# A depthwise-convolution and attention block on Trainium2: projection, token stage and attention placed on one hand-made memory map, and the norm sums taken from rounded halves

## What is computed

```python
hx = rms_norm(x, norm_g[l]) * (1.0 + scale[:, None, :]) + shift[:, None, :]
px = split_cols(hx @ w_in[l])          # q, k, v, g_att, c_a, c_b, g_conv, f_u, g_four
q, k = rope_2d(px[0]), rope_2d(px[1]); v = px[2]
attn = windowed_attention(q, k, v, kc, vc, attn_sink[l])
u = c_a * jax.nn.sigmoid(c_b)                                  # "glu"
y = depthwise_conv(u, conv_w, 31 taps) + conv_b
y_conv = jax.nn.silu(layer_norm(y, ln_g, ln_b))                # norm over 256 channels
y = concat([attn * silu(g_att), y_conv * silu(g_conv), y_four * silu(g_four)]) @ w_out
```

## Time and profile before

| what | value |
|---|---|
| median of 3 runs | 4472.19 us (4465.35 to 4475.61) |
| the profiled execution, time | 4470.44 us |
| its span in the trace | 4468.8 us |
| TensorE busy (PE) | 3851.7 us, 86% |
| VectorE busy (DVE) | 2926.1 us, 65% |
| ScalarE busy (ACT) | 1805.5 us, 40% |
| GpSimd busy (POOL) | 1454.0 us, 33% |
| mean granted clock of TensorE | 0.931 of full speed |

### The profile page before, as it was taken

One profiled execution on the slowest core, in us unless ns is written; L12 is line 12 of the kernel. 1 busy time (PEld: TensorE's weight loads), 2 busy tenths in 40 slices (PEclk: granted clock), 3 DMA queues, 4 the chain that ended last, 5 costly groups with the idle time before them and its releaser, 6 DMA issues. The chain is left out here.

```text
span 4468.8 us, 52488 instructions
## 1 busy us (share of the span) xinstructions
PE 3851.7 (86%) x18984; PEld 3168.4 (71%) x18984; DVE 2926.1 (65%) x3915; ACT 1805.5 (40%) x3069; POOL 1454.0 (33%) x1087
## 2 busy tenths in 40 slices
PE   4669998798796999879969689998989968887998
PEld 2558886687485888678847467777777767775886
DVE  2645943687375594368835687677766669995564
ACT  3332102676221210167722236554465455554331
POOL 1421110121121111012202155554445546664554
PEclk7779999899897999989989899999999989998999
DMA  6341122422474211242146423343333356555453
GB/s 239 107 162 62 71 80 81 108 60 57 160 251 143 76 71 75 76 115 64 48 150 221 173 90 118 118 157 112 115 116 123 109 151 152 153 142 175 169 193 116
DMA packets 332386, 554.01 MB, mean 124 GB/s; under 512 B 27382, under 2 KB 212470, under 8 KB 322584
## 3 DMA queue, kind: packets, MB, share of 16 engines
q1 hardware_dynamic: 304106, 442.06, 30.9%
q0 software_dynamic: 28032, 108.72, 6.6%
HBM read 397.69 MB, written 153.00 MB: 123 GB/s over the span
## 5 line engine op out<-in xcount | busy, mean ns | idle before, releaser
L2266 PE MATMUL in_ps<-in_h,in_wp 128*128 128x512 f32 x3792 | 914.1, 402 | 98.3 <-ACT in_h L2361 36.8
L2266 PEld LDWEIGHTS in_ps<-in_h,in_wp 128*128 128x128 f32 x3792 | 731.1, 194 | 275.7 <-issue 45.7
L1832 PE MATMUL out_ps<-out_y,out_wp 128*128 128x512 f32 x2976 | 689.5, 393 | 31.0 <-ACT out_y L1682 25.2
L1832 PEld LDWEIGHTS out_ps<-out_y,out_wp 128*128 128x128 f32 x2976 | 562.3, 189 | 157.6 <-issue 29.3
L495 PE MATMUL in_ps<-h,in_wp 128*128 128x512 f32 x2880 | 653.5, 389 | 0.7 <-POOL in_wp L667 0.7
L495 PEld LDWEIGHTS in_ps<-h,in_wp 128*128 128x128 f32 x2880 | 540.4, 188 | 113.8 <-POOL in_wp L667 1.5
L2230 POOL TENSOR_TENSOR in_wp<-in_w,in_wp 128x512 fp32r<-128x512 f32 x180 | 293.4, 1630 | 280.9 <-ACT in_wp L2345 280.6
L1747 POOL TENSOR_TENSOR out_wp<-out_w,out_wp 128x2048 fp32r<-128x2048 f32 (+1 forms) x48 | 193.0, 4021 | 406.5 <-ACT out_wp L1675 406.4
L634 DVE SCALAR_TENSOR_TENSOR cy<-cu,in_cw,cy 128x2048 f32<-128x2048 f32 x120 | 314.5, 2621 | 4.3
L972 PE MATMUL att_O<-att_pT,att_vs 128*128 128x512 f32 x960 | 302.0, 423 | 0.0
L2230 POOL TENSOR_TENSOR in_wp<-in_S,in_wp 128x512 fp32r<-128x512 f32 x132 | 218.8, 1658 | 228.5 <-ACT in_wp L2345 228.5
(11 more groups left out here) (502 smaller groups left out, 6993.6 us busy)
## 6 DMA issues: line engine op xcount, KB each, us to landing
in_w<-in_w_in SPq DMA_DIRECT2D x44, 1024.0 KB, 5.4
out_w<-in_w_out SPq DMA_DIRECT2D x32, 1024.0 KB, 4.8
out_mw<-in_w_ada_rows SPq DMA_DIRECT2D x48, 512.0 KB, 3.6
gates<-in_ob SPq DMA_DIRECT2D x40, 512.0 KB, 3.0
in_w<-in_w_in SPq DMA_DIRECT2D x36, 512.0 KB, 3.5
gates<-in_ob POOLq DMA_DIRECT2D x16, 1024.0 KB, 4.2
att_qf<-q SPq DMA_DIRECT2D x64, 256.0 KB, 4.4
out_yr<-y SPq DMA_DIRECT2D x16, 1024.0 KB, 6.7
```

Source lines behind the costliest of these rows:

```text
L1832: mm = nc.tensor.matmul(ps[:, u % NB, :W], wp[:, u % NW, a, k], y[:, c % 2, b, k], start=(i + k == 0), stop=(i == 2 and k == KY - 1))
L2266: mm = nc.tensor.matmul(ps[:, i % 2, bank], wp[:, g % RING, a, k], h[:, n, b, k], start=(first and part + k == 0), stop=(part == 2 and k = ...
```

## The change

The projection, the token stage and the attention of the 2048 rows get fixed addresses from one map (`SHARED`, `PROJECT`, `TOKENS`, `ATTENTION`), so that it is known which buffer of a stage lies over which of the stage before. With a plan, an engine enters the next stage (`early`) after fewer than five others have left, and the buffers that a stage frees early are the ones that the next stage loads first.

- `project`: written out without loops. The tiles come as sigmoid, glu, sigmoid, glu, six gates, four queries, one key, two gates. The first half of the convolution starts after the first glu tile; the second glu product is taken after tap `SECOND_AT` = 16. SyncE leaves after the last rotation, VectorE when the tile before the last has been stored, TensorE when all but the last tile are emptied.
- `tokens_conformer`: VectorE makes both halves of the weights. A sum over channels is now: VectorE adds the two halves of channels, rounds the sum (`totA`), subtracts (`totB`), and TensorE takes two matmuls of rounded operands. Sums, squares and Silu stand behind the tokens that four written-out lists name.
- `attention`: POOL issues the first keys, queries, mask and sink, VectorE makes both halves of the first ones; values and the rest are loaded by SyncE after it has left the token stage.
- Code of `project` for kinds of tiles that no call uses is removed. The columns of `w_in` are reordered on the host to fit.
- The context's stages get no plan, but run the same functions: unrolled, in the new order, with the new sums.

The core of the diff:

```diff
+HALF = 32768
+SHARED = placed((0, ("h", 4 * HALF), ("cy", 16384), ("cu", 16640)))
+PROJECT = placed((SHARED["cu"] + 16640, ("rot", 4096), ("w1", 4096), ("wp1", 8192), ("ob1", 8192), ("w0", 4096), ("wp0", 8192), ("ob0", 8192),
+                  ("cw31", 256), ("cb31", 32)))
+TOKENS = placed((SHARED["cu"], ("wA", 12288), ("w", 6144)), (SHARED["cu"] + 12288, ("tot", 2048), ("totA", 2048), ("totB", 2048)),
+                (PROJECT["w1"], ("wB", 12288), ("ob", 6144), ("root", 2048)),
+                (PROJECT["w0"], ("rstd", 4096), ("xh", 8192), ("sg", 8192)),
+                (PROJECT["cw31"] + 288, ("ones", 512), ("eps", 32), ("par", 32)))
+ATTENTION = placed((0, ("qf", 8192), ("qs", 8192), ("kf", 20480), ("kA", 20480), ("kB", 20480), ("mk", 7680), ("vf", 10240),
+                    ("ident", 512), ("nsink", 64), ("nm", 64), ("den", 64), ("sx", 64), ("rden", 64)),
+                   (3 * HALF, ("vs", 30720)),
+                   (4 * HALF, ("prob", 40960), ("pT", 16384), ("g", 4096), ("o", 4096), ("gR", 4096), ("wide", 4096)))
...
-                        with eng.Fori(start, end, 1) as i:
-                            for q in range(2):
-                                tile(i + at, q, kind, i * 2 + q, out, i * 2 + (n0 + q), scale)
...
+            def weights(t):
+                wait(sp, parted, t - 1)
+                sp.dma_start(wt[t % 2][:], w[t]).then_inc(w_in[t % 2], 16)
...
+            for t in range(2, total):
+                weights(t)
+            if rope:
+                sp.wait_ge(roped, kinds.count("rope"))
             s.leave(sp, "sync")
...
+            pe.wait_ge(emptied, total - 1)
...
+            def multiply(i):
+                t = [t for t in range(total) if kinds[t] == "glu"][i]
+                dve.wait_ge(mm_done, t + 1)
+                dve.wait_ge(emptied, t)
+                nc.vector.tensor_tensor(u[:, i, H:H + N], ps[:, t % 2, :N], y[:, i], ALU.mult).then_inc(multiplied, 1)
+            multiply(0)
+            dve.wait_ge(multiplied, 1)
+            dve.wait_ge(zeroed, 1)
+            dve.wait_ge(const_in, 32)
+            for i in range(2):
+                ts(y[:, i], u[:, i, 0:N], cw31[:, i, 0:1], cb31[:, i:i + 1], ALU.mult, ALU.add).then_inc(tapped, 1)
+                for k in range(1, CONV_K):
+                    dve.wait_ge(tapped, i * CONV_K + k)
+                    stt(y[:, i], u[:, i, k:k + N], cw31[:, i, k:k + 1], y[:, i], ALU.mult, ALU.add).then_inc(tapped, 1)
+                    if i == 0 and k == SECOND_AT:
+                        multiply(1)
+                if i == 0:
+                    dve.wait_ge(multiplied, 2)
...
+            late = total - 2
+            dve.wait_ge(mm_done, late + 1)
+            dve.wait_ge(parted, total)
+            dve.wait_ge(stored[late % 2], 16 * stores(late + 2))
+            dve.wait_ge(tapped, 2 * CONV_K)
...
+            if early:
+                keys(pool, 0)
+                queries(pool, 0)
+                keys(pool, 1)
+                pool.dma_start(mk[:], mask_d).then_inc(mask_in, 16)
+                pool.dma_start(nsink[:, 0], sink_d).then_inc(const_in, 16)
+                keys(pool, 2)
+                queries(pool, 1)
...
-            pool.wait_ge(const, 2)
-            pool.memset(vs[:, :, :, HD:2 * HD].bitcast(F32), 0.0).then_inc(padded, 1)
-            pool.wait_ge(padded, 1)
...
-            for b in range(2):
-                for half in range(2):
-                    rest(b, half)
+            for half in range(2):
+                rest(0, half)
+            s.join(pool)
+            s.clear(pool)
+            pool.memset(vs[:, :, :, HD:2 * HD].bitcast(F32), 0.0).then_inc(padded, 1)
+            pool.wait_ge(padded, 1)
+            for half in range(2):
+                rest(1, half)
...
+            if early:
+                s.join(sp, "vector", "scalar")
...
+            s.join(act, *(("scalar", "gpsimd") if early else ()))
...
+            if not early:
+                key_heads(0)
+                query_heads(0, 0)
+                query_heads(0, 1)
+                for p in range(1, FIRST):
+                    key_heads(p)
...
+            s.join(act, "sync")
...
+                if early and p < FIRST:
+                    dve.wait_ge(k_in[p], 32)
+                    nc.vector.tensor_copy(kA[:, :, c0:c1], kf[:, :, c0:c1]).then_inc(kled, 1)
...
+            def query_head(half):
+                q_loaded(dve, 0)
+                part = slice(half * GQ, (half + 1) * GQ)
+                nc.vector.tensor_copy(qs[:, 0, part], qf[:, 0, part]).then_inc(qled, 1)
             for p in range(FIRST):
                 key_rest(p)
+                if early and p == 0:
+                    query_head(0)
+                    query_head(1)
...
+    MEANS, VARS, SQUARES, SILUS = ((0, 1, 4, 6), (3, 5, 7, 9), (1, 2, 6, 8), (4, 6, 8, 10)) if NCH > 1 else ((0,), (1,), (1,), (2,))
+    SUMS = sorted([(t, "mean", c) for c, t in enumerate(MEANS)] + [(t, "var", c) for c, t in enumerate(VARS)])
...
+            pool.wait_ge(mm_done, max(NT - TW, 1))
...
-            pe.wait_ge(const, 2)
-            for c in range(min(2, NCH)):
-                means(c)
-            for t in range(max(NT, 3 * NCH + 1)):
+            def total(kind, c):
+                if nth(kind, c) == 1:
+                    s.join(pe, "scalar")
+                    pe.wait_ge(const, 2)
+                if kind == "mean":
+                    wait(pe, centred, c - 1)
+                else:
+                    wait(pe, rooted, c - 1)
+                pe.wait_ge(rested, nth(kind, c))
+                out = (psM if kind == "mean" else psV)[:, c % 2, :W]
+                nc.tensor.matmul(out, ones[:], totA[:], start=True, stop=False)
+                nc.tensor.matmul(out, ones[:], totB[:], start=False, stop=True).then_inc(summed, 1)
...
-                c = due(t, 3)
-                if c is not None:
-                    variances(c)
-                    if c + 2 < NCH:
-                        means(c + 2)
+                for at, kind, c in SUMS:
+                    if at == t:
+                        total(kind, c)
+            pe.wait_ge(centred, NCH)
+            pe.wait_ge(rooted, NCH)
...
+            if not early:
+                for k in range(KT):
+                    act.wait_ge(w_in[k % NWB], 16 * (k // NWB + 1))
+                    nc.scalar.activation(wA[:, k], wt[:, k % NWB], ACT.Copy).then_inc(led, 1)
...
-                c = due(t, 4)
-                if c is not None:
-                    silus(c)
-                    if c + 2 < NCH:
-                        square(c + 2)
+                if t in SQUARES:
+                    square(SQUARES.index(t))
+                if t in SILUS:
+                    silus(SILUS.index(t))
...
+                wait(dve, rested, n - 1)
+                tt(tot[:], two[0], two[1], ALU.add).then_inc(added, 1)
+                dve.wait_ge(added, n)
+                wait(dve, summed, n - 1)
+                nc.vector.tensor_copy(totA[:], tot[:]).then_inc(rounded, 1)
+                dve.wait_ge(rounded, n)
+                tt(totB[:], tot[:], totA[:].bitcast(F32), ALU.subtract).then_inc(rested, 1)
...
+                dve.wait_ge(rested, nth("var", c))
...
+            for k in range(KT):
+                if early:
+                    dve.wait_ge(w_in[k % NWB], 16 * (k // NWB + 1))
+                    nc.vector.tensor_copy(wA[:, k], wt[:, k % NWB]).then_inc(led, 1)
+                dve.wait_ge(led, k + 1)
+                tt(wB[:, k], wt[:, k % NWB], wA[:, k].bitcast(F32), ALU.subtract).then_inc(parted, 1)
+            dve.wait_ge(parted, KT)
+            gather("mean", 0)
+            if NCH > 1:
+                gather("mean", 1)
+            for c in range(min(2, NCH)):
+                centre(c)
+            gather("var", 0)
+            if NCH > 2:
+                gather("mean", 2)
+            for c in range(NCH):
+                invert(c)
+                if c + 1 < NCH:
+                    gather("var", c + 1)
+                gate(c)
+                if c + 2 < NCH:
+                    centre(c + 2)
+                if c + 3 < NCH:
+                    gather("mean", c + 3)
+            dve.wait_ge(mm_done, max(NT - TW, 1))
...
-                                    [("sigmoid", 2, None, 1.0), ("glu", 2, None, 1.0), (ACT.Silu, 8, gates, 1.0),
-                                     (turn, 4, q, -SCALE), (turn, 1, kout, 1.0)], source, tables=None if part else t["rope"],
...
+                    else:
+                        h, cy, cu = (chain.place(f"{a}{n}", shapes[a], F32R if a == "h" else F32, SHARED[a]) for a in ("h", "cy", "cu"))
+                    project(chain, f"in{n}", h, N, t["w_in"][l],
+                            [("sigmoid", 1, None, 1.0), ("glu", 1, None, 1.0), ("sigmoid", 1, None, 1.0), ("glu", 1, None, 1.0),
+                             (ACT.Silu, 6, gates[0:6], 1.0), (turn, 4, q, -SCALE), (turn, 1, kout, 1.0), (ACT.Silu, 2, gates[6:8], 1.0)],
```

(3 more changed lines are left out.)

531 lines of the change are left out of this document (198 added, 333 removed).

## The result

The changed kernel takes 4437.48 us (median of four runs, 4427.95 to 4439.67); the kernel before takes 4472.45 (four runs). The ratio is 0.992 with a 95% interval of 0.9901 to 0.9939, so 35.0 us are gone. The forecast was 4433.

The account below looks back on a forecast made before the run. Bound: TensorE's own work plus two seams per layer (barrier, load, split). Seams save 23.8 per layer, twice 47.6; the context returns 9: -38.6 on 4470.4 gives 4431.8, as median 4433; range 4408 to 4453, late split included.

Parts of the forecast that it names:

- First seam: Between projection and token stage: the gap goes whole, VectorE's split done at 688, last tile at 690.3, 2 us to spare.
- rival of the late split: At the first seam: tile 15's store or the loads come late, 5 to 10 us per layer stay, 4443 to 4453; 9%.
- Large projection: Main projection: the new order of tiles costs nothing; the second glu product is ready before tile 5 needs it.
- Three stalls: Token stage: TensorE waits before the variance sums of chunks 1 to 3 for VectorE's gather: 5.0, 6.2, 6.2 us, 17.4 in all.
- rival that the chain is short enough: Token stage: TensorE would not stall, another 23.4 us per layer and some 5 more, about 4376; 8%.
- Clock: Token stage: granted clock 0.50 after each stall, taken as 2.0 us per stall, 6.0 per layer, bounds 0 and 9.
- Second seam: Token stage to attention: POOL issues the loads early, first score 99.5 us behind the last projection matmul, before 124.3.
- Values late: Attention: values are loaded after SyncE's own last stores and ScalarE may want them earlier; costs 1 us per layer.
- Context: Context's small run of the same functions: gives back +9 us, with tile 5 starting 8.0 later for the second product.
- -2 for the ring: Context's projection: unrolled loops remove part of ScalarE's 8.0 us of sequencer waits, but weight loads bound the ring: -2 us.
- norm chain's +2: Context: the variance sum now waits for a gather and a later square, +2 us.
- POOL's issues blocked: Attention's door: twelve issues wait out VectorE's copy and subtraction, first score 32.6 us later per layer, 4498; rival, 5%.

Follow-up runs that it names:

- second profile of after: The kernel after, unchanged, timed and profiled once more beside later versions: 4437.8 us, ratio 0.9925; this profile's span is 4430.9.
- early-loads run: Kernel after, with POOL issuing its twelve attention loads before it stores the last result and waits for its landing: 4428.1 us, ratio 0.99.
- identity-first run: Kernel after with sums behind tokens 3, 6, 8, 10, early attention loads, early exponential table, POOL's identity and query split before its store wait: 4384.74 us, ratio 0.9809.
- reordered run: Kernel after, with variance sums behind tokens 3, 6, 8, 10 and ScalarE squaring for the next chunk between root and silus: 4405.56 us, ratio 0.9848.

## Why the prediction was right, point by point

The sum was -38.6, the median moved by -35.0, and in the profiles the touched part moved by -35.4. The mechanisms of the seams and of the new wait were right; two terms, the late values and the context, were sized wrongly, in opposite directions. Term by term:

- **First seam.** It was to go whole, with 2 us to spare. It left 0.26 us. VectorE was done with the sixteen operations at 685.0, 7.4 us before the projection's end in this profile, where 2 had been forecast: a copy took 0.35 us and a subtraction 0.56, against the bound of 0.68 for either. Putting the barrier back costs 20.6 us in layer 0 and 23.1 in layer 1. The rival of the late split did not occur.
- **Large projection.** Free, as forecast: from the main projection's first matmul to its last the two profiles have 373.9 and 374.2 us.
- **Three stalls.** Forecast 5.0, 6.2 and 6.2, measured 4.56, 5.70 and 6.17. The waits, their places and the releaser were as forecast, and the rival that the chain is short enough had no support. The version with full-float sums, which has no gather, has none of the three. By the Trainium skill, "VectorE: DVE Perf Modes", tier table, a float copy runs at twice the rate of a two-input operation. That was the better price for the copy, though the ratio here is under two: 512 columns took 0.43 us against the subtraction's 0.69, and 1152 columns 0.76 to 0.93 against 1.36. By its rule the forecast stalls would have been 4.7, 5.9 and 5.9.
- **Clock.** Forecast 6.0 us per layer, with 0 to 9 as bounds. The stage took 95.4 us; less 66.7 for the tokens, 3.6 for the sums and 16.4 for the stalls, 8.7 are left, which is taken for the clock by difference. The second profile of after had a mean clock of 0.91 over the stage instead of 0.89 and a stage of 93.2 us, which leaves 6.5. So the term was too small by 0.5 to 2.7 us.
- **Second seam.** First score forecast 99.5 us behind the last projection matmul, measured 102.8. (The 103.2 in the table above goes from the start of that matmul.) POOL's sixth issue ended at 93.7 instead of 91.7, since the last result was stored 2.2 us later than forecast. The second key piece took 6.7 us to land from there, where 5 was taken from a range of 3.3 to 6.9, and its copy was 0.4 us cheaper: +2.0, +1.7 and -0.4 are the 3.3. The nearest row in kind and size was the keys' own 6.9. Counted from the issue, as that row is, the median for these keys was 8.2 us in after, above the whole range. The prediction's sum for the query split is also off (95.9 and 2.49 are 98.4, not 97.9), without consequence, since the keys end later.
- **Values late.** Forecast 1 us per layer. First score to first value matmul grew by 3.1 and 5.7. This term failed. Two things were missing from it. ScalarE's table load of 1.28 us ran in before right behind its last key copy (813.12), and it then still waited 2.80 us for the first maximum; now it starts only when the maximum is there (798.00). And the values now end a store, a wait and a load behind the last token: SyncE fetches them at 799.01, 9.8 us behind the issue of its last store (2.8 us in the early-loads run), and ScalarE's value copy waits 3.11 us. In the identity-first run this chain is what takes back the earlier score.
- **Context.** Forecast +9, the largest error of a single term. The main projection began 1.8 us later in this profile, about 4 in the mean of ten. The step that failed is the price of a tap, 0.985 us, the mean of a group of thirty. VectorE's timeline of after has sixteen at 0.78 in the mean, and the second product 13.9 us behind the first, not 16.5:

```profile
104.09 0.98 DVE L535 TENSOR_SCALAR cyc<-cuc,inc_cw,inc_cb 128x256 f32<-128x256 f32 x1
...
105.12 12.49 DVE L538 SCALAR_TENSOR_TENSOR cyc<-cuc,inc_cw,cyc 128x256 f32<-128x256 f32 x16
...
117.52 0.42 DVE L528 TENSOR_TENSOR cuc<-inc_ps,cyc 128x256 f32<-128x256 f32 x1
```

  A tap has no single price. Narrower windows of the same timeline show one tap by itself, and then one beside a subtraction of POOL's:

```profile
105.12 0.48 DVE L538 SCALAR_TENSOR_TENSOR cyc<-cuc,inc_cw,cyc 128x256 f32<-128x256 f32 x1
...
105.58 2.40 POOL L585 TENSOR_TENSOR inc_wp<-inc_w,inc_wp 128x1024 fp32r<-128x1024 f32 x1 [0.65 <-ACT inc_wp L474]
105.64 2.62 DVE L538 SCALAR_TENSOR_TENSOR cyc<-cuc,inc_cw,cyc 128x256 f32<-128x256 f32 x1
```

  Two of POOL's subtractions lie beside those sixteen taps (16 x 0.48 + 2 x 2.4 = 12.5, and 12.49 were measured), seven beside the thirty of the kernel before. The price was the mean over another mix. So tile 5 began at 122.15, not 125.5, 4.6 later than before instead of 8.0, and TensorE's pause was 6.32 us, not 8 to 10. The -2 for the ring held: the last matmul was 2.6 later than before, so 2.0 of the 4.6 were made up. That this is the unrolled loop is likely, not shown: in the run with the product behind the third tap ScalarE's copies waited 3.0 us for its own sequencer, not 8.0 (5.5 + 2.5 in the earlier trace rows). The norm chain's +2 did not cost anything: TensorE waits 2.44 us before the context's variance sum, but from the projection's last matmul to the first context score are 42.5 us, 43.8 before.
- **POOL's issues blocked.** They took 0.55 to 0.73 us each in after, and at most 0.78 in the early-loads run, where they lie beside copies of keys and queries on VectorE. By the page of the Trainium skill, "SBUF — State Buffer", section on the two separate sides, a DMA issued by POOL takes 3100 ns beside a float copy instead of 620. The early-loads run has the two side by side and does not show it.

Twice 23.8 were to come from the seams, and 18.4 and 17.7 did (21.5 and 23.4 at the first score, less 3.1 and 5.7 behind it); the context took back 2 to 4 instead of 9. Errors of 11 and of 5 to 7 us cancelled for the most part: the total was closer than its terms, and that part of the agreement is luck.

## What to carry to other kernels

A cheaper instruction on the bounding engine is no gain if what prepares it is queued behind a long chain on another: the rounded sums saved TensorE 1.25 us each and cost 12 to 15 us per layer until the order of squares, sums and roots was changed, which made the kernel 1.5% faster than before instead of 0.8%. A mean time of an instruction is a price only for the same company on the other engines: the tap's 0.985 us was 0.48 by itself and 2.62 beside a subtraction of POOL's. When two stages are overlapped, write down for every engine what its queue holds at the seam and which store has to land first; here the bound went from keys to POOL's wait for a store to the round trip of the values, and each fix was worth only the distance to the next. The best version of this case, reordered and with early loads, takes 4382 to 4385 us, about 2% less than before.

## What was not expected of the hardware

- VectorE and POOL stand in each other's way when both work inside SBUF. In the context's projection a tap of VectorE's waits out POOL's subtraction whole, and POOL keeps its pace (2.62 us for a tap of 0.48, 2.40 for the subtraction, above). Elsewhere both are slowed. In the identity-first run, VectorE's timeline has the 1152-column subtraction that takes 1.36 us alone, and an eight-column operation that takes 0.17 alone:

```profile
762.71 2.33 DVE L1016 TENSOR_TENSOR att_kB<-att_kf,att_kA 128x1152 fp32r<-128x1152 f32 x1
765.19 1.03 DVE L1077 TENSOR_SCALAR att_nsink<-att_nsink 128x8 f32<-128x8 f32 x1
```

and POOL's, over the same time, two query subtractions that take 2.50 alone:

```profile
762.14 4.05 POOL L831 TENSOR_TENSOR att_qs<-att_qf,att_qs 64x512 fp32r<-64x512 f32 x2
```

- A store lands late when loads were issued before it: POOL's store of 512 columns landed after some 4 us by itself, and after 9.5 to 9.8 behind twelve loads on the same queue. Whether the queue or the traffic on the DMA engines does it was not separated.
- Equal code can get another clock from run to run: an untouched group of 48 matmuls in the second layer ran at 0.50 in the reordered run and in the one with the context's product behind the third tap (10.34 us each), and at 1.00 in both profiles of after (5.52 and 5.47). The first of these runs has hardly any stalls left in its token stage and the second has all of them, so the stalls do not decide it; what does is open.
